# Memory's values computed behind the experts, x's queries first, and a new order in retention

## The reference, cut to what matters

```python
# first block
xn = rms_norm(h, norm_mix_g);  proj = xn @ w_in        # sb_q, sb_k, sb_v, r_q, r_k, r_v, r_g
y_sb = stick_breaking_attention(sb_q, sb_k, sb_v) @ w_sb_out
scores = einsum('bhncd,bhnmd->bhncm', qc, kc) * d_intra    # retention, 8 heads, decays d_intra
...                                                        # values, states of the chunks, norm
y_ret = (silu(r_g) * y_ret) @ w_ret_out
h = h + (g_sb * y_sb + g_ret * y_ret) @ w_out              # g: sigmoid(xn @ w_gate + b_gate)
h = h + hierarchical_moe(rms_norm(h, norm_ffn_g), ...)     # 16 experts, two a token
x = rms_norm(h, norm_final_g)
# second block
h = rmsnorm(x, norm_mix_g_2); ...                          # sparse and dilated attention
m = rmsnorm(mem_2, norm_mem_g_2)                           # memory: 256 tokens
kvc = m @ w_kv_cross                                       # first half: keys, second half: values
sc = einsum('bshd,bmhd->bhsm', qc, keys) * 256 ** -0.5
oc = einsum('bhsm,bmhd->bshd', softmax(sc), values)
...                                                        # o_cross, an MLP, the final norm
```

## Time and profile before

| | |
|---|---|
| median of 3 runs | 1719.45 us |
| the profiled execution | 1720.16 us |
| its span, first to last instruction | 1718.3 us |
| TensorE busy | 1634.2 us |
| VectorE, ScalarE, GpSimd busy | 937.8, 745.6, 608.5 us |
| mean granted TensorE clock | 0.983 |

### The profile page before, as it was taken

How to read it: one execution, slowest core, us unless ns; L and a number is a source line. 1 busy time by engine, 2 the same in 40 slices (tenths; PEclk the granted TensorE clock), 3 DMA queues, 4 the chain that set the end, 5 groups by cost and what they waited for, 6 DMA issues and landing times.

```text
span 1718.3 us, 21081 instructions
## 1 busy us (share of the span) xinstructions
PE 1634.2 (95%) x8000; PEld 1327.9 (77%) x8000; DVE 937.8 (55%) x1122; ACT 745.6 (43%) x895; POOL 608.5 (35%) x255
## 2 busy tenths in 40 slices
PE   8999999899999899999968989899999999999996
PEld 8888888658886878888857858766886888888885
DVE  6524310377174589999966679894433553231414
ACT  6344413234334577888854142475324322222221
POOL 1332154313434122232222616564431444444441
PEclk9999999999999999999989989999999999999998
DMA  7321034312223699999963314300321222222221
GB/s 260 125 74 50 25 111 133 112 37 98 98 103 112 233 414 421 404 389 390 393 244 119 103 49 139 110 1 1 132 89 50 93 79 100 96 98 98 98 98 49
DMA packets 46739, 250.30 MB, mean 146 GB/s; under 512 B 9456, under 2 KB 10224, under 8 KB 19920
## 3 DMA queue, kind: packets, MB, share of 16 engines
q1 hardware_dynamic: 40912, 238.89, 37.3%
q0 software_dynamic: 5184, 8.40, 1.4%
q10 hardware_dynamic: 576, 2.10, 0.3%
HBM read 239.20 MB, written 14.68 MB: 148 GB/s over the span
## 4 chain that ended last, share of the span: by engine, by line
PE 72%; issue 11%; DVE 7%; POOL 3%; DMA 3%; ACT 2%; SPq 1%; ACTq 0%; DVEq 0%; POOLq 0%
PE psum L229 21%; PE psum L231 20%; PE psum L230 20%; POOL w_lo L148 3%; PE psum L2175 2%; PE psum L2208 1%; DVE kept_bias L2062 1%; PE psum L718 1%; DVE top L2061 1%; PE psum L2196 1%; PE psum L2442 1%; DVE kept_bias L2054 1%; PE psum L1284 1%; ACT w_hi L142 1%; PE psum L737 1%
## 5 line engine op out<-in xcount | busy, mean ns | idle before, releaser
L148 POOL TENSOR_TENSOR w_lo<-raw,w_hi 128x2048 fp32r<-128x2048 f32 x93 | 428.4, 4606 | 739.8 <-ACT w_hi L142 704.5
L229 PE MATMUL psum<-x_hi,w_hi 128*128 128x512 f32 x840 | 330.1, 393 | 6.3 <-DVE w_lo L148 4.8
L230 PE MATMUL psum<-x_lo,w_hi 128*128 128x512 f32 x840 | 327.8, 390 | 0.0
L231 PE MATMUL psum<-x_hi,w_lo 128*128 128x512 f32 x840 | 327.8, 390 | 0.0
L142 ACT ACTIVATE w_hi<-raw 128x2048 fp32r<-128x2048 f32 x100 | 190.9, 1910 | 314.8 <-PE psum L231 311.0
L1302 DVE TENSOR_TENSOR moe_lo<-moe_w,moe_hi 128x2048 fp32r<-128x2048 f32 x99 | 225.7, 2290 | 37.0 <-ACT moe_hi L1292 35.1
L1292 ACT ACTIVATE moe_hi<-moe_w 128x2048 fp32r<-128x2048 f32 x99 | 189.3, 1915 | 36.8 <-PE psum L231 19.7
L229 PEld LDWEIGHTS psum<-x_hi,w_hi 128*128 128x128 f32 x840 | 158.3, 188 | 42.0 <-DVE w_lo L148 5.2
L230 PEld LDWEIGHTS psum<-x_lo,w_hi 128*128 128x128 f32 x840 | 158.3, 188 | 33.4 <-issue 0.7
L231 PEld LDWEIGHTS psum<-x_hi,w_lo 128*128 128x128 f32 x840 | 158.2, 188 | 33.1
L432 DVE TENSOR_TENSOR res<-res,psum 128x512 f32<-128x512 f32 x56 | 38.4, 687 | 217.6 <-PE psum L231 217.6
(11 more groups left out here) (370 smaller groups left out, 2889.0 us busy)
## 6 DMA issues: line engine op xcount, KB each, us to landing
raw<-in_w_dense SPq DMA_DIRECT2D x101, 1024.0 KB, 4.8
moe_w<-in_w_moe_ahead SPq DMA_DIRECT2D x54, 1024.0 KB, 14.6
moe_w<-in_w_moe SPq DMA_DIRECT2D x48, 1024.0 KB, 14.1
yrow<-expert_rows SPq DMA_DIRECT2D x8, 512.0 KB, 7.1
res<-in_x SPq DMA_DIRECT2D x4, 512.0 KB, 9.0
decay<-in_decay SPq DMA_DIRECT2D x8, 256.0 KB, 3.8
hn_rows<-hn_tok ACTq DMA_DIRECT2D x4, 512.0 KB, 4.6
out<-res SPq DMA_DIRECT2D x4, 512.0 KB, 2.6
```

Source lines behind the costliest of these rows:

```text
L148: pool.tensor_tensor(w_lo[c % RING][:, :], raw[c % RING][:, :], w_hi[c % RING][:, :].bitcast(F32), ALU.subtract).then_inc(lo_ready, 1)
L229: pe.matmul(out, lh, rh, start=first, stop=False)
L230: pe.matmul(out, lh, rl, start=False, stop=False)
L231: return pe.matmul(out, ll, rh, start=False, stop=last)
```

## The change

- v_mem is no dense layer any more. Its four chunks are put behind the last pair in the array of expert chunks loaded ahead (w_moe_ahead gets a ninth entry: four chunks of values' weights and two of zeros), and a register expression picks that entry in the last round's last pair. They go through the experts' ring, and all four are split there.
- Memory normed for k_mem (m_high, m_low) is stored to DRAM after the layer "out" and read back (vm_hi, vm_lo) when the last pair has released slot 7. The root mean square by memory token (two matmuls, a root, a reciprocal, the scale in L2371) goes.
- Memory's values are computed in combine: three chunks (six tiles) before the first transposes, the fourth between the transposes of blocks 1 and 2. ScalarE evacuates the eight tiles (v_mem_out) in between its other work there and issues the two stores. sums(q) come one block later; some buffers move.
- The start: x is loaded first. Queries and keys both use x with the gain but without the norm, VectorE evacuates both; sb_v alone uses the normed x. VectorE and ScalarE do x's splits first, the squares and additions behind them. The norm's sum stands behind the second tile of queries.
- Retention: values of a pair's first head stand ahead of the next pair's scores. Four buffers for the decays; those of heads 2 and 3 are loaded behind gate_sb's chunks.
- Route: the split of the third expert chunk stands behind k_mem's last evacuations.

```diff
-LAYERS = [("v_mem", 4), ("sb_q", 2), ("sb_k", 2), ("sb_v", 2), ("ret_v", 4), ("ret_q", 2), ("ret_k", 2),
+LAYERS = [("sb_q", 2), ("sb_k", 2), ("sb_v", 2), ("ret_v", 4), ("ret_q", 2), ("ret_k", 2),
...
+        for g in range(4):
+            if g == 1:
+                load_chunk(sp, 0)
+            sp.dma_start(res[:, 2 * g:2 * g + 2, :], d["x"][:, 2 * g:2 * g + 2, :]).then_inc(x_landed[g], 16)
         load_chunk(sp, 1)
-        for g in range(4):
-            if g == 2:
-                load_chunk(sp, 2)
-            sp.dma_start(res[:, 2 * g:2 * g + 2, :], d["x"][:, 2 * g:2 * g + 2, :]).then_inc(x_landed[g], 16)
+        load_chunk(sp, 2)
         for name, tile in CONSTS:
             sp.dma_start(tile[:, :], d[name]).then_inc(consts_landed, 16)
         load_chunk(sp, 3)
-        dense_sync(sp, "v_mem")
-        sp.wait_ge(bank_free, FIRST_TILE["v_mem"] + KT + 4)
-        sp.dma_start(vc_rows, vc_out[:, :, :]).then_inc(v_moved, 16)
         for name in ("sb_q", "sb_k", "sb_v"):
             dense_sync(sp, name)
...
+        def key(j):
+            dve.wait_ge(tile_done, FIRST_TILE["sb_k"] + j + 1)
+            dve.tensor_tensor(sb_k[:, j, :], psum[:, (FIRST_TILE["sb_k"] + j) % 4, :], norm1.rstd[:, :], ALU.mult)\
+               .then_inc(bank_free, 1)
         x_low(0)
         x_low(1)
-        norm1.add_square(dve, 2)
+        first_low(0, first_high_done, first_low_done)
         x_low(2)
-        split_lo(dve, 2)
-        norm1.add_square(dve, 3)
         x_low(3)
-        norm1.add_square(dve, 4)
-        x_low(4)
-        split_lo(dve, 3)
+        first_low(1, hi_ready, lo_ready)
+        for kt in range(4, KT):
+            x_low(kt)
+        for kt in range(1, 5):
+            norm1.add_square(dve, kt)
+        split_lo(dve, 1)
         for kt in range(5, KT):
             norm1.add_square(dve, kt)
-            x_low(kt)
         norm1.vector_invert(dve)
+        norm1.wait_inverted(dve)
+        dve.wait_ge(bank_free, 4)
+        for j in range(3):
+            query(j)
         for g in range(4):
             dve.wait_ge(x_landed[g], 16)
...
         x_high(0)
         x_high(1)
-        square(2)
+        act.wait_ge(raw_landed[0], 16)
+        first_high(0, first_high_done)
         x_high(2)
-        v_mem_out(1)
+        x_high(3)
+        first_high(1, hi_ready)
+        for kt in range(4, KT):
+            x_high(kt)
+        for kt in range(5):
+            norm1.square(act, kt)
+        split_hi(act, 1, 0)
+        for kt in range(5, KT):
+            norm1.square(act, kt)
         split_hi(act, 2, 2)
-        square(3)
-        x_high(3)
-        v_mem_out(2)
-        square(4)
-        x_high(4)
-        v_mem_out(3)
-        split_hi(act, 3, 4)
-        for kt in range(5, KT):
-            square(kt)
-            x_high(kt)
-        v_mem_out(4)
-        v_mem_out(5)
-        split_hi(act, 4, 6)
-        v_mem_out(6)
-        v_mem_out(7)
         norm1.act_root(act)
-        split_hi(act, 5, 8)
         for kt in range(3):
             norm_high(kt)
-        split_hi(act, 6, 10)
+        split_hi(act, 3, 4)
         for kt in range(3, KT):
             norm_high(kt)
-        split_hi(act, 7, 12)
-        dense_act(act, "sb_k", lambda e, i, j, bank: e.activation(
-            sb_k[:, j, :], psum[:, bank, :], ACT.Copy).then_inc(bank_free, 1))
+        dense_act(act, "sb_k")
...
-        for _ in range(30):
+        for _ in range(24):
             pe.matmul(psum[:, 7, 0:P], ones[:, :], ones[:, :], start=True, stop=True)
 
         class FirstParts:
             def wait_split(self, pe, n):
-                pe.wait_ge(mv_low, n)
+                pe.wait_ge(u_low, n)
                 if n == 1:
-                    pe.wait_ge(v_first_low, 1)
+                    pe.wait_ge(first_low_done, 1)
                 if n == 5:
                     pe.wait_ge(lo_ready, 1)
-        dense_pe(pe, "v_mem", mv_hi, mv_lo, token_major=True, norm=FirstParts(), by_parts=True,
-                 hooks={3: lambda: norm1.pe(pe)})
-        dense_pe(pe, "sb_q", u_hi, u_lo, norm=Parts(u_low))
-        dense_pe(pe, "sb_k", x_hi, x_lo, norm=norm1)
-        dense_pe(pe, "sb_v", x_hi, x_lo, token_major=True)
+        dense_pe(pe, "sb_q", u_hi, u_lo, norm=FirstParts(), by_parts=True, tile_hooks={1: lambda: norm1.pe(pe)})
+        dense_pe(pe, "sb_k", u_hi, u_lo)
+        dense_pe(pe, "sb_v", x_hi, x_lo, token_major=True, norm=norm1)
...
-    dec = [at(f"decay{b}", 186 + 2 * b, [P, S]) for b in range(2)]
+    dec = [at(f"decay{b}", kb, [P, S]) for b, kb in enumerate((186, 188, 110, 108))]
+    DECAY_AT = (0, 1, 2, 3, 0, 1, 2, 0)
+    DECAY_NTH = (1, 1, 1, 1, 2, 2, 2, 3)
...
+    def retention_more_decays(sp):
+        rot1.wait(sp, "ret_k", 1)
+        for h in range(2, 4):
+            sp.dma_start(dec[h][:, :], d["decay"][h]).then_inc(r_landed[h], 16)
+
     def retention_sync(sp):
-        for h in range(2, HEADS):
-            sp.wait_ge(rp_done, h - 1)
-            sp.dma_start(dec[h % 2][:, :], d["decay"][h]).then_inc(r_landed[h % 2], 16)
+        for h, b in ((4, 0), (5, 1), (6, 2), (7, 0)):
+            sp.wait_ge(rp_done, 5 if h == 7 else h - 3)
+            sp.dma_start(dec[b][:, :], d["decay"][h]).then_inc(r_landed[b], 16)
...
         scores(0)
         for h in range(HEADS):
+            values(h)
             if h % 2 == 0 and h + 2 < HEADS:
                 scores(h // 2 + 1)
-            values(h)
...
         dense_sync(sp, "out")
+        norm_mem.wait_split(sp)
+        sp.dma_start(m_rows[0], m_high[:, :, :].bitcast(F32)).then_inc(m_stored, 16)
+        sp.dma_start(m_rows[1], m_low[:, :, :].bitcast(F32)).then_inc(m_stored, 16)
...
-        pe.wait_ge(n_added, (KT - 1) * (norm_mem.u + 1))
-        for m in range(MEM // P):
-            mm = pe.matmul(psum[:, 6, m:m + 1], norm_mem.sum[:, m * P:(m + 1) * P], ones[:, 0:1], start=(m == 0),
-                           stop=True, skip_group_check=True)
-        mm.then_inc(mem_tok_summed, 1)
...
-            moe_split_chunk(act, 0, 2)
...
             hooks={0: lambda: [rows(2), rows(3), gate_exps()], 2: first_experts}, ahead=False)
+        moe_split_chunk(act, 0, 2)
         moe_rows_high(act, 0, 1)
...
     def moe_sync(sp):
+        n_rounds = rounds_of(sp)
         sp.wait_ge(kv_moved, 16)
-        sp.wait_ge(v_moved, 16)
+        sp.wait_ge(m_stored, 32)
         sp.wait_ge(credits, 1)
 
         def body(n, i, r):
@@ -1554,13 +1507,17 @@
                   .then_inc(moe_landed[s // 2], 16)
             for s in range(MOE_AHEAD):
                 sp.wait_ge(moe_used, MOE_RING * n + MOE_RING + s + 1)
-                sp.dma_start(ring[s][:, :], d["w_moe_ahead"][bass.ds(i, 1), s].rearrange("a p n -> p (a n)"))\
+                ahead = i + ((n + (4 * PAIRS + 1) - n_rounds * PAIRS) >> 5 & 1)
+                sp.dma_start(ring[s][:, :], d["w_moe_ahead"][bass.ds(ahead, 1), s].rearrange("a p n -> p (a n)"))\
                   .then_inc(moe_landed[s // 2], 16)
-        n_rounds = expert_loop(sp, body)
+        expert_loop(sp, body, n_rounds)
+        for t, rows in ((vm_hi, m_rows[0]), (vm_lo, m_rows[1])):
+            sp.wait_ge(moe_used, n_rounds * (MOE_RING * PAIRS) + 8)
+            sp.dma_start(t[:, :, :].bitcast(F32), rows).then_inc(vm_landed, 16)
         for s in range(MOE_AHEAD // 2):
             sp.wait_ge(moe_landed[s], n_rounds * (32 * PAIRS) + 32)
             sp.sem_inc(wait_seen, 1)
-        sp.wait_ge(moe_low, n_rounds * (MOE_RING * PAIRS) + 3)
+        sp.wait_ge(moe_low, n_rounds * (MOE_RING * PAIRS) + V_CHUNKS)
...
+        pe.wait_ge(tr_ev[1], rounds_read[0] * (2 * PAIRS) + 2)
+        pe.sem_inc(wait_seen, 1)
+        pe.wait_ge(vm_landed, 32)
+
+    def v_mem_tensor(pe, s):
+        pe.wait_ge(moe_low, rounds_read[0] * (MOE_RING * PAIRS) + s + 1)
+        wh, wl = (t[:, :].rearrange("p (m k n) -> p m k n", k=KT, n=P) for t in (ring_hi[s % MOE_HI], ring_lo[s]))
+        for m in range(MEM // P):
+            j = 2 * s + m
+            if j >= 2:
+                pe.wait_ge(v_read, j - 1)
+            for kt in range(KT):
+                mm = three_pass(pe, psum[:, 7 * (j % 2), 0:2 * P], vm_hi[:, kt, m * P:(m + 1) * P],
+                                vm_lo[:, kt, m * P:(m + 1) * P], wh[:, :, kt, :], wl[:, :, kt, :], kt == 0, kt == KT - 1)
+            mm.then_inc(v_done, 1)
...
-        expert_loop(act, body)
+        n_rounds = expert_loop(act, body)
+        moe_split_chunk(act, n_rounds * PAIRS, 3)
...
+        def v_mem_out(j):
+            s, m = j // 2, j % 2
+            act.wait_ge(v_done, j + 1)
+            act.activation(vc_out[m][:, 256 * s:256 * s + 256], psum[:, 7 * (j % 2), 0:256], ACT.Copy).then_inc(v_read, 1)
+        for j in range(3):
+            v_mem_out(j)
         gated(0)
+        v_mem_out(3)
         gated(1)
+        v_mem_out(4)
+        v_mem_out(5)
         squared(0)
+        gated(2)
+        v_mem_out(6)
+        v_mem_out(7)
         high(0)
-        gated(2)
+        act.wait_ge(v_read, 8)
```

(11 more changed lines are left out.)

102 lines of the change are left out of this document (30 added, 72 removed).

## The result

| | before | changed | ratio, 95% interval |
|---|---|---|---|
| first measurement, 5 runs each | 1720.61 us | 1708.41 us (1703.44 to 1709.67) | 0.9921 [0.99, 0.9941] |
| the same kernel once more, 6 runs | 1721.21 us | 1706.41 us (1702.08 to 1710.64) | 0.9918 [0.9901, 0.9935] |
| profiled execution, span | 1718.3 us | 1701.6 us | |

The changed kernel is 12 to 15 us faster, where 26.5 were forecast: the sign is right, the size is not, and 1708.4 lies outside the range 1687 to 1700.5. The profiled execution (1703.44 us) is the lowest of the first five: it gained 16.7 us, and the median lies 5 us above it. So two things are to be explained: 9.8 us that are missing in the profile itself, and what the other executions lose against it, in a spread of 6 to 9 us (4 to 7 us for the kernel before, over as many runs or more).

A forecast was written before the change was run, and what follows sets the result against it. TensorE, busy in 95% of the span, was taken as the bound, so gains come from removed work or filled holes. 27.3 + 1.2 + 3.0 - 5.0 = 26.5 us off the median 1719.45 gave 1693.0 us, range 1687 to 1700.5.

The forecast's parts named there:

- Part 1, the start: Start up to sb_v: memory's values leave it, sb_v starts at 55.4 instead of 82.66; 27.3 us gained, bounds 22.9 and 29.
- Rival (a): Start: x and chunk 0 arrive late, TensorE starts at 13 and waits for the norm's sum; 1697.5 us, chance 0.12.
- Part 2, retention: Retention: values(0) start 4.0 us earlier, decays lie ready; 1.2 us gained, bounds 4.0 gained and 1 lost.
- from there each pair loses a little, 0.5 to 0.8: Retention after values(2): scores between even and odd head's values push back the odd head's mean square and root.
- Part 3, mix and route: Mix to experts: removed matmuls 0.3 and ScalarE's order 3.2 gained, memory's stores 0.5 lost; together 3.0 us gained.
- I charge 0.5 us; bounds 0 and 3: Route: cost of storing 2.1 MB of normed memory, delaying hn's rows and the first expert loads.
- Rival (f): Route: memory's stores hold up the rows of hn by the whole 3 us; 1695.5 us, chance 0.05.
- the two sums I made there: Route: stores' price, 0.5 us from 1.7 us spilling over, or by the skill's shared-engines rule the full 3 us.
- Part 4: Experts and behind: pairs unchanged at 35.5 us; memory's values fill the hole, last chunk hidden; 5.0 us lost, bounds 3 and 10.7.
- rival (d): Expert loop: SyncE's register expressions delay the weight loads, 38 us over 8 pairs; time 1731, chance 0.03.
- (b): Combine: the last chunk of memory's values is not hidden, 10.7 us lost instead of 5.0; 1698.7 us, chance 0.14.
- (e): Behind the experts: memory's values start near 886 and don't fill the hole, 5 us more lost; 1698 us, chance 0.06.

The follow-up runs named there:

- experiment 2: Changed kernel with only retention's TensorE order put back (next pair's scores ahead of values of a pair's first head), four decay buffers kept: 1703.57 us.
- 8: Changed kernel with memory's stores early, SyncE's k_mem store wait moved to chunk 10, root's table loaded before retention, scores mostly behind the mean square: 1694.73 us.
- experiment 3: Changed kernel with one extra ScalarE root at the head of retention, so that the root's table is loaded in idle time: 1702.79 us.
- experiment 5: Experiment 4's kernel with two decay buffers again instead of four: 1698.79 us.
- experiment 4: Changed kernel with memory's two 1 MB stores put ahead of the loads of layer out on SyncE: 1697.23 us, ratio to before 0.9861.
- 6: Experiment 4's kernel with the first expert's chunk 2 split on ScalarE inside k_mem again, behind its fifth tile: 1700.26 us.
- experiment 9: Experiment 4's kernel with three quarters of the memory values' matmuls left out (v_mem wrong): 1697.82 us.
- experiment 13: Four more profiles of the unedited changed kernel, to find a slower execution: 1701.5, 1703.85, 1700.5 and 1704.33 us.
- experiment 12: Kernel of experiment 8 with the first expert's chunk 0 to 2 loads no longer held for hn's first two row stores: 1691.9 us, ratio 0.9834.
- experiment 10: Changed kernel with early memory stores and SyncE's k_mem wait at chunk 10, plus chunk 0 to 2 loads held for all four hn stores: 1698.44 us.

## Why the prediction was wrong, step by step

**Part 1, the start: right.** 26.25 us against 27.3. The queries' first matmul came at 10.18 (I had 9.7) and sb_v's at 56.40 (55.4). Rival (a) did not happen. No experiment tested this part; it rests on the two traces.

**Part 2, retention: wrong in its sign.** Forecast 1.2 gained, bounds 4.0 gained and 1 lost; measured 2.74 lost. The first steps came true (values(0) 4.0 us nearer, values(2) 2.4 instead of 2.9). The step that failed is "from there each pair loses a little, 0.5 to 0.8". A part of the 2.4 is only borrowed: scores(2) stood ahead of values(2) and now stand behind them, so both pairs up to values(6) contain scores where one did. And the scores between values(h) and mean_square(h-1) lie on the cycle of values, copy, square and root. A pair without scores takes 8.5 us, one with scores on that cycle 10.9, one with scores behind the mean square 9.8. So the first pair lost 1.1 us and the second 2.4, against 2.4 gained: 1.1 lost, where 1.2 gained was forecast. On top I counted no fall of the clock, which costs 1.65 us in three of the six profiled executions; where it does not fall, retention takes 44.8 us, just past the bound of 1 lost. Experiments 2 and 8 show the order's part, experiment 3 the table load's 1.4. The decay buffers, to which I gave part of the gain, bring nothing in this order (experiment 5); in the old one they remove an idle of 1.1 us (experiment 2).

**Part 3, mix and route: the term that failed most.** Forecast 3.0 gained, measured 3.06 lost (0.39 - 3.45). The removed matmuls and the split of the third chunk were sized right: without the stores the route gained 2.35 us (experiment 4), and with the split back this is gone (6). What failed is "I charge 0.5 us; bounds 0 and 3" for the stores: 48.4 - 42.6 = 5.8 us in the profiled executions, and 9.2 us by the medians. Of them, 4.3 are TensorE's wait for the gathered rows and 1.6 the clock behind it; the 3.4 us that the medians show beyond that are in no trace. Rival (f) named the place and was given 0.05; even its 3 us were half of the price. I worked out how many bytes spill over (1.7 us), as if the row stores would only be late by that. They are the first of four transfers that wait for each other, with 3 MB of loads released by the first of them.

The row of the changed kernel's chain is hn_rows 10.16 us, on ScalarE's queue, while memory's stores and the loads that it met were on SyncE's. The Trainium skill, "DMA: Bandwidth & Descriptors", section "Issuing engines are not separate DMA queues", says that all issuing engines' transfers share the 16 DMA engines and interleave. This trace agrees, with those 10.16 us just behind the three loads, where experiment 4, in which the loads leave 6.5 us sooner, has 4.9 at most; and of the two sums I made there the one by that rule came nearer.

**Part 4.** The experts' pairs stayed at 35.4 us, and rival (d) is out. I had not counted the first pair: it lost 0.9 us, as chunk 6's load left later behind TensorE's start. The combine cost 4.08 us to the keys' first matmul, 42.65 behind the last expert matmul (I said 43 to 45; 38.57 before), and 1.2 us came back in what follows; 5.0 was 1 to 2 too much. The mechanism was right: the first transposes are 4.5 us later behind the last expert matmul (17.69 against 13.16), and from them to the keys TensorE takes 24.96 us against 25.41, so the fourth chunk is hidden; experiment 9 agrees. Rivals (b) and (e) did not happen.

**The sum.** 26.25 - 2.74 + 0.39 - 3.45 - 0.88 - 4.08 + 1.2 = 16.7 us. Of the 9.8 us missing against the forecast, 3.9 are retention's, 6.1 the route's, 0.9 the first pair's, 1.1 the start's, less 2.1 at the combine and behind it. The other 5 us between the profile and the median are not fully explained. The collision of the stores does not account for the spread: with the stores moved, the four runs of experiment 4 lie within 3 us, but those of experiments 5, 6 and 9, which have them moved too, spread over 5.3, 6.4 and 5.7 us, and the four of experiment 3, which has not, over 1.9. Two things that differ between executions are seen in the profiles (the clock in retention, 1.6 us; k_mem's store close behind chunks 3 to 5, up to 5). But none of the six profiled executions of the changed kernel took more than 1704.3 us (experiment 13), so what the ones above 1705 lose stays open, and also whether a profiled execution is quicker by itself (those of the other kernels are not: 1702.21 us was the highest of four in experiment 5). So does why the clock fell to 0.61 in some executions and not in others behind the same idle of 2.4 us.

## What to carry to other kernels

A transfer's price is not its bytes but what waits for the transfers that it meets: walk the chain of small, waited-for transfers and ask which large ones are issued between its links. Two 1 MB stores on such a chain cost 5.8 us in the profile; that three loads are best put ahead of the whole chain (experiment 12) is likely but not shown. In a loop of several engines, look which work stands between an instruction and the one that the cycle returns through; the same scores made a pair 2.4 us longer on one side of a mean square and 1.3 on the other. And what comes earlier in one place because work was moved behind it has to be paid there. Where a stage gains and the end does not, follow one anchor per stage until the gain is gone; that place, not the stage, is next. And check where a gain arrives, not only its size: in experiment 9 the size came out and the place did not.

## What the runs showed of the hardware

A 1 MB store issued 4.1 us behind 3 MB of loads took 12.1 us to land (experiment 5), one issued 8.9 us behind them 6.3 (before): 4.8 us sooner, 5.8 us longer. In windows full of loads, 35 and 7 us long, the engines moved 421 and 423 GB/s. A 0.5 MB store took 2.6 to 4.9 us where no large transfer was issued close to it (experiments 4 and 10), and up to 11.2 beside three 1 MB loads (12). In retention the granted clock fell behind one idle of 2.4 us, to a mean of 0.61 over 4 us in the changed kernel's first profile, between its levels of 1.2 and 2.4 GHz; in other executions of the same program, behind the same idle, it stayed at 1.00: three times each in six. Behind 3.4 us it fell in experiment 2, and in the kernel before it did not.
